# The shared expert's down weights in a two-layer MoE decoder step: a slot of the down ring at passes 24 and 25 instead of passes 1 and 2

## The chip, the core and the metric

The kernel runs on one core of a Trainium2 chip. A core has five engines that run their own instruction streams and meet through semaphores: TensorE (PE in the rows; PEld are its weight loads), VectorE (DVE), ScalarE (ACT), GpSimd (POOL) and SyncE (SP), which here only issues transfers. Weights lie in HBM and are brought into SBUF by DMA; matmul results go to PSUM. The metric is the device time of one execution in microseconds (us), lower is better.

## What is computed

One inference step of a decoder trunk of two layers, for 256 prompt tokens and 8 x 8 sample tokens (320 in all, width 1024). Each layer has a token mixer (window attention in layer 0, gated linear attention in layer 1) and then a mixture of experts, which takes most of the time:

```python
scores = sigmoid(x @ router_w)                       # 64 experts
... group-limited top 8 of 64 -> eidx, weights w
routed = sum over the 8 chosen e: w_e * (silu(x @ wg[e]) * (x @ wu[e])) @ wd[e]
shared = (silu(x @ swg) * (x @ swu)) @ swd           # one expert that every token uses
return routed + shared
```

An expert has a gate-and-up matrix (wg and wu, 1024 x 512 together, 2 MiB in float32) and a down matrix (wd, 256 x 1024, 1 MiB). The shared expert has the same sizes: shared_up is its gate and up, **shared_down** (swd) its down matrix. All 64 experts are loaded once per layer.

## The kernel before

**Passes.** Experts are sorted by how many tokens they drew and run in 28 passes per layer, two or three experts side by side in a pass (`PASSES`; passes 1, 2, 7, 13, 16, 21, 26 and 27 hold three). `LOAD_ORDER` numbers the 64 experts in the order of the passes; "item 34" below is number 34 of that order, counted from 0. Pass 14 holds items 32 and 33, pass 15 items 34 and 35, pass 24 items 54 and 55, pass 25 items 56 and 57, pass 26 items 58 to 60, pass 27 items 61 to 63. In a pass TensorE does the gate-and-up product (L2029), a part of the token gathering for the next batch of passes (L1931), turns the hidden values (L2055), adds the pass before into the sums of the tokens (L1959, L1961), and does the down product (L2079). Its last down product raises `y_full`.

**Rings.** Gate-and-up weights go through a ring of six slots (`gu_ring`), down weights through a ring of five (`dn_ring`, `NDN = 5`). A slot may be loaded again when the pass that read it is done: `gu_full` frees slots of the first ring, `y_full` those of the second.

**Who issues.** SyncE issues all gate-and-up loads in the order of the passes (L1612); each waits for its slot. SyncE also issues the first down loads (L1596 for items 0 and 1, L1615 for items below `DN_EARLY`) and those of the last pass (L1621). All other down loads are issued by ScalarE (L2127), at the end of the pass that frees the slot, behind that pass's two copies of the down result (L2121). So there are two hardware queues: SyncE's (q1) with the 2 MiB loads, ScalarE's (q10) with the 1 MiB loads, and each serves its loads in order.

**The shared expert.** Its gate and up run before the passes (L1723). Its down weights are loaded by SyncE (L1603) while the routing is computed, into the fifth slot of the down ring; only four slots are left for early items (`DN_EARLY = 4`). Its down product, in three parts of 128, 128 and 64 tokens (`shared_down`, L2007), runs in passes 1 and 2: the first part behind the down product of pass 1, the other two between the gate-and-up product and the turning of pass 2. The last part raises `shd_used`, and item 8 may then take the slot. From item 9 on, item i takes the slot of item i - 5.

Of the kernel before, what the change touches and what calls it, by code (L numbers as in the profile page):

```python
# [40 lines left out]
GH, DK, DV = 4, 128, 256  # L41
NE, FF = 64, 256
NGRP = 8
NGU, NDN, DN_EARLY = 6, 5, 4
DN_PLACE = (3, 4, 0, 1, 2)
NFIX = 2
EPS = 1e-6
# [43 lines left out]

PASSES = [pass_plan(l) for l in range(2)]
NP = len(PASSES[0])
BATCHES = (2, 4, 4, 4, 4, 4, 4, 2)
BATCH_OF = [(q, j) for q, n in enumerate(BATCHES) for j in range(n)]
BATCH_START = [sum(BATCHES[:q]) for q in range(len(BATCHES))]
# [144 lines left out]
def decoder_step(nc, a, debug=None):  # L241
    with ExitStack() as ctx:
# [25 lines left out]
        lay, const_range, _ = const_layout()  # L268
# [1294 lines left out]
        order = sb("order", [P, NE], I32)  # L1563
        excess = sb("excess", [P, 2], I32)
        last_dn = [None] * NDN
        gu_of, dn_of = {}, {}

        def expert_slots(l):

            for r in LOAD_ORDER[l]:  # L1570
                s = units[0] % NGU
                units[0] += 1
                i = LOAD_ORDER[l].index(r)
                d = i % DN_EARLY if i < 2 * DN_EARLY else (i + 1) % NDN
                used = (S["shd_used"], l + 1) if i == 2 * DN_EARLY else None if i < DN_EARLY else last_dn[d]
                slot_in[s].n += 16
                down_in[d].n += 16
                gu_of[(l, r)] = (s, slot_in[s].n, last_item[s])
                dn_of[(l, r)] = (d, down_in[d].n, used)
                last_item[s] = (S["gu_full"], l * NP + pass_of[l][r] + 1)  # L1580
                last_dn[d] = (S["y_full"], 2 * (l * NP + pass_of[l][r] + 1))

        def expert_stream(l, dn_ring):

            w_up, wd = a["moe_up"][l], a["moe_wd"][l]

            @block.sync
            def _(sp):
                if l == 0:
                    sp.wait_ge(*attention_read[0])  # L1590
                else:
                    sp.wait_ge(*states_out[0])
                    stored.wait(sp)
                for r in range(NFIX):
                    d = dn_of[(l, r)][0]
                    sp.dma_start(dn_ring[:, DN_PLACE[d], :], wd[r].rearrange("(p f) n -> p (f n)", p=P)).then_inc(down_in[d].h, 16)  # L1596
                for r in range(NFIX):
                    s, _, used = gu_of[(l, r)]
                    sp.wait_ge(*used)
                    sp.dma_start(gu_ring[:, s, :], w_up[r]).then_inc(slot_in[s].h, 16)  # L1600
                normed(sp, 2 * l + 1)
                stored.wait(sp)
                sp.dma_start(dn_ring[:, DN_PLACE[NDN - 1], :], a["shared_down"][l]).then_inc(down_in[NDN - 1].h, 16)  # L1603
                sp.wait_ge(S["order_full"], l + 1)
                for i, r in enumerate(LOAD_ORDER[l]):
                    if i < NFIX:
                        continue
                    e = sp.value_load(order[0:1, r:r + 1], min_val=0, max_val=NE - 1)
                    s, _, used = gu_of[(l, r)]
                    if used:  # L1610
                        sp.wait_ge(*used)
                    sp.dma_start(gu_ring[:, s, :], w_up[e]).then_inc(slot_in[s].h, 16)  # L1612
                    if i < DN_EARLY:
                        d = dn_of[(l, r)][0]
                        sp.dma_start(dn_ring[:, DN_PLACE[d], :], wd[e].rearrange("(p f) n -> p (f n)", p=P)).then_inc(down_in[d].h, 16)  # L1615

                for r, _ in PASSES[l][NP - 1]:
                    e = sp.value_load(order[0:1, r:r + 1], min_val=0, max_val=NE - 1)
                    d, _, used = dn_of[(l, r)]
                    sp.wait_ge(*used)  # L1620
                    sp.dma_start(dn_ring[:, DN_PLACE[d], :], wd[e].rearrange("(p f) n -> p (f n)", p=P)).then_inc(down_in[d].h, 16)  # L1621
# [14 lines left out]
        def moe(l):  # L1636
            with ExitStack() as c:
                dn_ring = sb("dn_ring", [P, NDN, DNW], c=c)
                down_in[NDN - 1].n += 16
                shd_n = down_in[NDN - 1].n  # L1640
                expert_slots(l)
                expert_stream(l, dn_ring)
                htok = sb("htok", [P, 2, 2, D], F32R, c=c)
                htok2 = sb("htok2", [P, D], F32R, c=c)
# [3 lines left out]
                ovh = sb("ovh", [P, 2, T], c=c)  # L1648
                sg_, sg_n = shared_in[l]
                shw = item(sg_)  # L1650
                shd = dn_ring[:, DN_PLACE[NDN - 1], :].rearrange("p (f n) -> p f n", f=2)

                def step(ins):
                    settled(nc.vector, ins)
# [268 lines left out]
                def _(pe):  # L1923
# [87 lines left out]
                    for p in range(NP):  # L2011
# [31 lines left out]

                        turns = list(enumerate(fills))
                        fill_some(turns[:3])
                        if p == 2:
                            shared_down(1, (0,))
                            shared_down(1, (1,))
                            shared_down(2, (0, 1)).then_inc(S["shd_used"], 1)
# [23 lines left out]
                        for half in range(2):  # L2073
# [5 lines left out]
                                    last = pe.matmul((W1, W2)[half][o:o + n, :], hTs[:, f, o:o + n],  # L2079
                                                     dn_ring[:, DN_PLACE[dn_of[(l, r)][0]], w0:w0 + 512], start=(f == 0), stop=(f == 1))  # L2080
                            last.then_inc(S["y_full"], 1)
                        if p == 1:
                            pe.wait_ge(down_in[NDN - 1].h, shd_n)
                            shared_down(0, (0,))
                            shared_down(0, (1,))
                    rest_pe(pe, left)
# [4 lines left out]
                def _(act):  # L2091
# [15 lines left out]
                    for p in range(NP):  # L2107
                        if p == NP - 1:
                            left = any_left(act)
                        q = BATCH_OF[p][0]  # L2110
                        act.wait_ge(S["gu_full"], l * NP + p + 1)
                        act.activation(sg[:, :], W0[:, 0:FF], ACT.Silu).then_inc(S["silu_full"], 1)  # L2112
                        for f in fills_in(p)[::2]:
                            fill_out(q + 1, f)
                        act.wait_ge(S["tr_full"], l * (NP + 1) + p + 2)
                        act.copy(hTs[:, :, :], W0[:, 0:FF].rearrange("p (f s) -> p f s", s=P)).then_inc(S["hT_full"], 1)  # L2116
                        if last_of(p):
                            weights_out(q + 1)
                        for half in range(2):
                            act.wait_ge(S["y_full"], 2 * (l * NP + p) + half + 1)  # L2120
                            act.copy(yhi[:, half, :], (W1, W2)[half]).then_inc(S["y_high"], 1)  # L2121
                        for r in LOAD_ORDER[l][DN_EARLY:len(LOAD_ORDER[l]) - len(PASSES[l][NP - 1])]:
                            d, _, used = dn_of[(l, r)]
                            if used == (S["y_full"], 2 * (l * NP + p + 1)) or (p == 2 and used == (S["shd_used"], l + 1)):
                                e = act.value_load(order[0:1, r:r + 1], min_val=0, max_val=NE - 1)
                                act.wait_ge(*used)
                                act.dma_start(dn_ring[:, DN_PLACE[d], :], a["moe_wd"][l][e].rearrange("(p f) n -> p (f n)", p=P)).then_inc(down_in[d].h, 16)  # L2127
# [466 lines left out]
```

## Time and profile before

| | us |
|---|---|
| median of 3 runs (1441.85 to 1442.69) | 1442.52 |
| the profiled execution | 1440.6 |
| its span in the profile | 1438.8 |
| busy TensorE in the span | 1397.9 (97%) |
| busy VectorE, ScalarE, GpSimd | 437.5, 317.1, 48.1 |
| passes of layer 0, first gate-and-up product to last down product | 247 to 707 |
| passes of layer 1 | 956 to 1418 |

The span is what the profile covers; the execution's time is 1.8 us longer. TensorE is busy nearly all the time, and so are the DMA engines during the passes, so busy shares alone do not tell which of the two sets the end. That is read from the waits, from the times of single transfers, and from the bytes moved in a stretch.

### The profile page before, as it was taken

The page shows a single profiled execution, that of the slowest core. Times are in us where ns is not written, and L with a number is a line of the kernel's source. Part 1 is how long each engine was busy: PE and PEld are TensorE (multiplying, and loading weights), DVE is VectorE, ACT ScalarE, POOL GpSimd, SP SyncE. Part 2 cuts the span into 40 slices and gives each one's busy share as a digit, 9 for nine tenths or more (in the row PEclk, how much of TensorE's full clock was granted, in tenths as well). Part 3 has the DMA queues.
Part 4 walks back from the last instruction along what each step waited for, and adds up shares of the span by engine and source line. Part 5 has one row for each costly group of instructions (what it writes and reads, how often), then busy time and mean ns, then how long its engine had stood idle before and what let it go on. Part 6 is the DMA issues. An engine that isn't in the chain of part 4 may idle for free.

```text
span 1438.8 us, 20775 instructions
## 1 busy us (share of the span) xinstructions
PE 1397.9 (97%) x8288; PEld 707.9 (49%) x8288; DVE 437.5 (30%) x1161; ACT 317.1 (22%) x746; POOL 48.1 (3%) x86
## 2 busy tenths in 40 slices
PE   7999999999999999999999999999999999999997
PEld 3345656444444444544465456564444445444433
DVE  1146435312221222221345143442122212132114
ACT  2134323111111111111345122411111111111113
POOL 0100301000000000000100010010000000000000
PEclk9999999999999999999999999999999999999999
DMA  9999528999999999999972246289999999999992
GB/s 392 386 383 427 218 94 321 391 402 427 411 424 427 419 426 426 423 427 425 406 298 118 117 161 239 91 361 404 405 427 417 425 420 422 425 425 424 426 419 88
DMA packets 48003, 509.52 MB, mean 354 GB/s; under 512 B 5809, under 2 KB 6209, under 8 KB 8321
## 3 DMA queue, kind: packets, MB, share of 16 engines
q1 hardware_dynamic: 27728, 370.42, 61.9%
q10 hardware_dynamic: 16416, 119.54, 20.1%
q0 software_dynamic: 3760, 18.20, 3.4%
q8 instruction: 68, 1.11, 0.3%
q14 instruction: 31, 0.25, 0.0%
HBM read 499.10 MB, written 11.01 MB: 355 GB/s over the span
## 4 chain that ended last, share of the span: by engine, by line
PE 87%; DMA 5%; DVE 3%; ACT 3%; issue 1%; ACTq 0%; SPq 0%; DVEq 0%
PE bank L2029 25%; PE banks L2079 13%; PE banks L1931 10%; PE banks L442 5%; DMA s_dn_ring<-in_moe_wd_dram 4%; PE ybank L1959 3%; PE banks L1119 3%; PE banks L1959 3%; PE bank L1961 3%; PE bank L504 2%; PE ybank L1723 1%; PE banks L1723 1%; DMA s_gu_ring<-in_ada_w_dram 1%; PE banks L697 1%; PE banks L1124 1%; PE banks L671 1%
## 5 line engine op out<-in xcount | busy, mean ns | idle before, releaser
L2029 PE MATMUL bank<-s_gu_ring,s_hbuf 128*32 128x512 f32 (+1 forms) x2688 | 395.3, 593 | 0.9 <-DVE s_hbuf L2160 0.9
L2029 PEld LDWEIGHTS bank<-s_gu_ring,s_hbuf 128*32 128x32 f32 (+1 forms) x2688 | 122.2, 119 | 264.7 <-issue 264.7
L2079 PE MATMUL banks<-s_dn_ring,s_hTs 128*32 128x512 f32 (+1 forms) x1344 | 205.9, 602 | 4.9 <-DMA s_dn_ring<-in_moe_wd_dram 4.9
L2205 DVE TENSOR_TENSOR s_ylo<-banks,s_yhi 128x512 fp32r<-128x512 f32 x112 | 77.5, 692 | 327.0 <-ACT s_yhi L2121 327.0
L1931 PE MATMUL banks<-s_sel,s_htok 128*128 128x512 f32 (+1 forms) x640 | 144.8, 374 | 0.5 <-issue 0.5
L1931 PEld LDWEIGHTS banks<-s_sel,s_htok 128*128 128x128 f32 x640 | 106.3, 188 | 60.7 <-issue 44.3
L2121 ACT CAST s_yhi<-banks 128x512 fp32r<-128x512 f32 x112 | 65.7, 586 | 303.3 <-PE banks L2079 303.3
L2079 PEld LDWEIGHTS banks<-s_dn_ring,s_hTs 128*32 128x32 f32 (+1 forms) x1344 | 56.8, 119 | 123.9 <-issue 123.2
L2200 DVE SCALAR_TENSOR_TENSOR s_hh<-s_sg,s_wsl,bank 128x256 f32<-128x256 f32 x56 | 26.9, 480 | 287.2 <-ACT s_sg L2112 287.2
L2112 ACT ACTIVATE s_sg<-bank 128x256 f32<-128x256 f32 x56 | 21.6, 385 | 364.0 <-PE bank L2029 364.0
L2160 DVE COPY s_hbuf<-banks 128x512 f32<-128x512 f32 (+1 forms) x60 | 39.4, 656 | 96.0 <-PE banks L1931 96.0
L1119 PE MATMUL banks<-s_gu_ring,s_hbuf 128*128 128x512 f32 x128 | 55.9, 593 | 0.5 <-DVE s_rs L1439 0.5
L2095 ACT COPY s_hbuf<-banks 128x512 f32<-128x512 f32 (+1 forms) x60 | 33.5, 559 | 57.9 <-PE banks L1931 57.9
L1959 PE MATMUL ybank<-s_yhi,s_gt 128*128 128x512 f32 x108 | 38.7, 439 | 0.0
L1119 PEld LDWEIGHTS banks<-s_gu_ring,s_hbuf 128*128 128x128 f32 x128 | 24.2, 191 | 29.1 <-issue 28.2
L504 PE MATMUL bank<-s_gu_ring,s_condT 128*32 128x512 f32 x288 | 35.5, 605 | 0.6 <-DMA s_gu_ring<-in_ada_w_dram 0.6
L2116 ACT COPY s_hTs<-bank 128x256 f32<-128x256 f32 x56 | 20.9, 373 | 64.0 <-PE bank L2055 43.1
L442 PE MATMUL banks<-s_qk,s_gu_ring 128*128 128x320 f32 x128 | 34.9, 433 | 0.0
L442 PE MATMUL banks<-s_hbuf,s_gu_ring 128*128 128x320 f32 x128 | 34.9, 433 | 0.0
L1959 PE MATMUL ybank<-s_ylo,s_gt 128*128 128x512 f32 x108 | 33.9, 395 | 0.0
L1959 PE MATMUL banks<-s_yhi,s_gt 128*128 128x512 f32 x108 | 33.9, 395 | 0.0
L1959 PE MATMUL banks<-s_ylo,s_gt 128*128 128x512 f32 x108 | 33.6, 392 | 0.0
(463 smaller groups left out, 1452.9 us busy)
## 6 DMA issues: line engine op xcount, KB each, us to landing
s_gu_ring<-in_moe_up_dram SPq DMA_DIRECT2D x128, 2048.0 KB, 16.2
s_dn_ring<-in_moe_wd_dram ACTq DMA_DIRECT2D x114, 1024.0 KB, 17.0
s_gu_ring<-in_ada_w_dram SPq DMA_DIRECT2D x24, 2048.0 KB, 14.3
s_dn_ring<-in_moe_wd_dram SPq DMA_DIRECT2D x14, 1024.0 KB, 11.2
s_gu_ring<-in_win_dram SPq DMA_DIRECT2D x6, 2048.0 KB, 12.0
s_gu_ring<-in_wqkv_dram SPq DMA_DIRECT2D x6, 1024.0 KB, 19.5
s_gu_ring<-in_wo_dram SPq DMA_DIRECT2D x2, 2048.0 KB, 20.5
s_gu_ring<-in_shared_up_dram SPq DMA_DIRECT2D x2, 2048.0 KB, 10.7
```

The lines of the kernel that those rows point to most:

```text
L442: last = pe.matmul(b[:, 0:T], item(slot)[:, k, (m % 4) * P:(m % 4 + 1) * P], src[:, k, :], start=(k == 0), stop=(k == KC - 1))
L504: last = pe.matmul(ada_bank(n)[32 * j:32 * j + 32, :], condT[:, k, lo:lo + 32], item(s)[:, k, :], start=(x == 0 and kk == 0), stop=(ends_g ...
L1119: last = pe.matmul(b[:, :], hT[:, k, t0:t0 + P], w[:, k, :], start=(k == 0), stop=(k == KC - 1))
L1931: last = pe.matmul(b[:, width * x:width * x + width], w[:, m * P:(m + 1) * P], sel[:, s, 0:width], start=(n == 0), stop=(n == 4))
L1959: last = pe.matmul(acc[(t, half)], g[:, t * P:(t + 1) * P], y[:, half, :], start=(p == 0 and y is yhi), stop=False)
L1961: last = pe.matmul(bank[6][:, :], g[:, 320 - 64 * half:448 - 64 * half], y[:, half, :], start=(p == 0 and y is yhi and half == 0), stop=False)
L2029: last = pe.matmul(W0[o:o + n, :], tokens_of(p, k)[:, o:o + n], w[:, k, :, :], start=(k == 0), stop=(k == KC - 1))
L2079: last = pe.matmul((W1, W2)[half][o:o + n, :], hTs[:, f, o:o + n], dn_ring[:, DN_PLACE[dn_of[(l, r)][0]], w0:w0 + 512], start=(f == 0), st ...
L2095: act.copy(fill_target(q, f), fill_source(q, f)).then_inc(S["fill_act"], 1)
L2121: act.copy(yhi[:, half, :], (W1, W2)[half]).then_inc(S["y_high"], 1)
L2160: dve.tensor_copy(fill_target(q, f), fill_source(q, f)).then_inc(S["fill_dve"], 1)
L2205: dve.tensor_tensor(ylo[:, half, :], (W1, W2)[half], yhi[:, half, :].bitcast(F32), ALU.subtract).then_inc(S["y_low"], 1)
```

## The change

The shared expert's down weights become an item of the down ring. They stand behind the experts of passes 0 to 24 (ahead of item 56), take the slot of item 51, and are issued by ScalarE at the end of pass 22. Their products run in pass 24 (first part, behind its down product) and pass 25 (the other two). All five slots are free for early items: item 4 is now issued early by SyncE. Items 56 to 60 each take the slot of the ring's entry five places before, so item 60 waits for the last product of the shared expert (`shd_used`), and ScalarE issues it at the end of pass 25.

```diff
-NGU, NDN, DN_EARLY = 6, 5, 4
+NGU, NDN, DN_EARLY = 6, 5, 5
...
+SHD_PASS = 24
...
+            shd_at = sum(len(experts) for experts in PASSES[l][:SHD_PASS + 1])
             for r in LOAD_ORDER[l]:
...
-                d = i % DN_EARLY if i < 2 * DN_EARLY else (i + 1) % NDN
-                used = (S["shd_used"], l + 1) if i == 2 * DN_EARLY else None if i < DN_EARLY else last_dn[d]
+                if i == shd_at:
+                    d = i % NDN
+                    down_in[d].n += 16
+                    shd_of.append((d, down_in[d].n, last_dn[d]))
+                    last_dn[d] = (S["shd_used"], l + 1)
+                d = (i + (i >= shd_at)) % NDN
+                used = None if i < NDN else last_dn[d]
...
-                sp.dma_start(dn_ring[:, DN_PLACE[NDN - 1], :], a["shared_down"][l]).then_inc(down_in[NDN - 1].h, 16)
...
-                        if p == 2:
+                        if p == SHD_PASS + 1:
                             shared_down(1, (0,))
                             shared_down(1, (1,))
                             shared_down(2, (0, 1)).then_inc(S["shd_used"], 1)
...
-                        if p == 1:
-                            pe.wait_ge(down_in[NDN - 1].h, shd_n)
+                        if p == SHD_PASS:
+                            pe.wait_ge(down_in[shd_d].h, shd_n)
                             shared_down(0, (0,))
                             shared_down(0, (1,))
...
+                        if shd_of[l][2] == (S["y_full"], 2 * (l * NP + p + 1)):
+                            act.wait_ge(*shd_of[l][2])
+                            act.dma_start(dn_ring[:, DN_PLACE[shd_d], :], a["shared_down"][l]).then_inc(down_in[shd_d].h, 16)
                         for r in LOAD_ORDER[l][DN_EARLY:len(LOAD_ORDER[l]) - len(PASSES[l][NP - 1])]:
                             d, _, used = dn_of[(l, r)]
-                            if used == (S["y_full"], 2 * (l * NP + p + 1)) or (p == 2 and used == (S["shd_used"], l + 1)):
+                            if used == (S["y_full"], 2 * (l * NP + p + 1)) or (p == SHD_PASS + 1 and used == (S["shd_used"], l + 1)):
```

TensorE, layer 0, in the kernel before: the end of pass 1 (L2079) and the first half of pass 2. L2007 is the shared expert's down product.

```order
L2079 MATMUL banks<-s_dn_ring,s_hTs 32x512 x16
L2007 MATMUL ybank<-s_dn_ring,s_ovh 128x512 x4
L2029 MATMUL bank<-s_gu_ring,s_hbuf 32x512 x32
L1931 MATMUL banks<-s_sel,s_htok 128x512 x4
L1931 MATMUL banks<-s_sel,s_htok_0 128x512
...
L2007 MATMUL banks<-s_dn_ring,s_ovh 128x512 x4
L2007 MATMUL bank<-s_dn_ring,s_ovh 64x512 x4
L2055 MATMUL bank<-s_cst,s_hh 128x128 x2
```

In the changed kernel the two L2007 places are gone here: L2029 follows L2079, and L2055 follows L1931.

TensorE, layer 0, in the changed kernel: the end of pass 24 and the first half of pass 25. The same lines have other numbers there: L2085 is the down product, L2013 the shared expert's, L2035 gate-and-up, L1937 the gathering, L2061 the turning.

```order
L2085 MATMUL banks<-s_dn_ring,s_hTs 64x512 x8
L2013 MATMUL ybank<-s_dn_ring,s_ovh 128x512 x4
L2035 MATMUL bank<-s_gu_ring,s_hbuf 64x512 x16
L1937 MATMUL banks<-s_sel,s_htok 128x256 x4
L1937 MATMUL banks<-s_sel,s_htok_0 128x256
...
L2013 MATMUL banks<-s_dn_ring,s_ovh 128x512 x4
L2013 MATMUL bank<-s_dn_ring,s_ovh 64x512 x4
L2061 MATMUL bank<-s_cst,s_hh 128x128 x2
```

The three products moved as they are, by 23 passes.

ScalarE, layer 0, in the changed kernel: the end of pass 22 and all of pass 23. L2127 copies the down result, L2134 reads the expert's number, L2130 and L2136 issue down loads.

```order
L2127 CAST s_yhi<-banks 128x512 x2
L2130 DMA s_dn_ring<-in_shared_down_dram 128x2048
L2134 TENSOR_LOAD s_order
L2134 ISA x2
L2136 ISA
L2136 DMA s_dn_ring<-in_moe_wd_dram 128x2048
L2118 ACTIVATE s_sg<-bank 128x256
L2101 COPY s_hbuf<-banks 128x256
L2122 COPY s_hTs<-bank 128x256
```

In the kernel before, this place issues items 55 and 56; now it issues the shared expert's weights and, behind them, item 55.

## Rows read from the trace of the kernel before

**Rows 1.** The page, part 1: engine, busy us, share of the span, instructions.

```profile
PE 1397.9 (97%) x8288; PEld 707.9 (49%) x8288; DVE 437.5 (30%) x1161; ACT 317.1 (22%) x746; POOL 48.1 (3%) x86
```

**Rows 2.** TensorE's waits, whole span: who waited for whom, us, times, longest.

```profile
PE banks L2079 <- DMA s_dn_ring<-in_moe_wd_dram: 4.9, 2, 2.5
```

**Rows 3.** Timeline of TensorE at pass 26 of both layers: start, us, instruction, [idle before <- releaser].

```profile
690.12 3.64 PE L2079 MATMUL banks<-s_dn_ring,s_hTs 128*32 128x512 f32 x32 [2.42 <-DMA s_dn_ring<-in_moe_wd_dram]
...
1399.23 1.82 PE L2079 MATMUL banks<-s_dn_ring,s_hTs 128*32 128x512 f32 x8 [2.52 <-DMA s_dn_ring<-in_moe_wd_dram]
```

**Rows 4.** The chain that ended last: start, us, what; the longest transfer in layer 0.

```profile
663.78 26.21 DMA s_dn_ring<-in_moe_wd_dram
```

**Rows 5.** Timeline of TensorE, layer 0, end of pass 1 and pass 2.

```profile
282.51 3.70 PE L2007 MATMUL ybank<-s_dn_ring,s_ovh 128*128 128x512 f32 x8
286.14 7.07 PE L2029 MATMUL bank<-s_gu_ring,s_hbuf 128*32 128x512 f32 x64
...
295.56 3.59 PE L2007 MATMUL banks<-s_dn_ring,s_ovh 128*128 128x512 f32 x8
...
300.96 0.50 PE L2055 MATMUL bank<-s_cst,s_hh 128*128 128x128 f32 x2
```

**Rows 6.** SyncE in layer 0: the shared expert's early load, and item 63's load.

```profile
214.74 0.33 SPq L1603 DMA_DIRECT2D s_dn_ring<-in_shared_down_dram  x1
...
L1621 SPq DMA_DIRECT2D s_dn_ring<-in_moe_wd_dram x1: 338/338/338, 694.0 to 694.0; - x1
...
DMA to landing us min/median/max: 4.9/4.9/4.9
```

**Rows 7.** Timeline of TensorE: the down products of passes 24, 25 (layer 0) and 24 (layer 1).

```profile
658.34 3.65 PE L2079 MATMUL banks<-s_dn_ring,s_hTs 128*64 128x512 f32 x16
...
673.85 3.65 PE L2079 MATMUL banks<-s_dn_ring,s_hTs 128*64 128x512 f32 x16
...
1367.37 3.65 PE L2079 MATMUL banks<-s_dn_ring,s_hTs 128*64 128x512 f32 x16
```

**Rows 8.** Windows of layer 0: busy us of each engine, granted clock, DMA share, GB/s.

```profile
252.00:260.00 8.00, 8.00 (x38) 4.91 (x36) 1.65 (x3) 1.83 (x4) 0.00 (x0) 1.00 0.88 339
264.00:280.00 16.00, 16.00 (x118) 9.06 (x112) 2.65 (x7) 2.06 (x5) 0.00 (x0) 1.00 0.96 385
308.00:316.00 8.00, 8.00 (x70) 3.01 (x63) 1.39 (x4) 0.83 (x2) 0.00 (x0) 1.00 0.91 339
316.00:640.00 324.00, 324.00 (x2047) 151.99 (x2046) 77.52 (x189) 50.76 (x105) 0.00 (x0) 1.00 1.01 423
```

**Rows 9.** The DMA view from 547 to 691 us: packets, MB, mean rate.

```profile
DMA packets 5634, 61.18 MB, mean 425 GB/s; under 512 B 631, under 2 KB 631, under 8 KB 631
```

**Rows 10.** Single down loads of layer 0, items 33, 34, 41, 55: issue time, us to landing.

```profile
L2127 ACTq DMA_DIRECT2D s_dn_ring<-in_moe_wd_dram x1: 345/345/345, 471.4 to 471.4; - x1
...
DMA to landing us min/median/max: 10.1/10.1/10.1
...
L2127 ACTq DMA_DIRECT2D s_dn_ring<-in_moe_wd_dram x1: 345/345/345, 487.6 to 487.6; - x1
...
DMA to landing us min/median/max: 11.1/11.1/11.1
...
L2127 ACTq DMA_DIRECT2D s_dn_ring<-in_moe_wd_dram x1: 345/345/345, 535.7 to 535.7; - x1
...
DMA to landing us min/median/max: 11.7/11.7/11.7
...
L2127 ACTq DMA_DIRECT2D s_dn_ring<-in_moe_wd_dram x1: 344/344/344, 633.1 to 633.1; - x1
...
DMA to landing us min/median/max: 19.5/19.5/19.5
```

**Rows 11.** The same of layer 1: item 34.

```profile
L2127 ACTq DMA_DIRECT2D s_dn_ring<-in_moe_wd_dram x1: 344/344/344, 1196.6 to 1196.6; - x1
...
DMA to landing us min/median/max: 11.3/11.3/11.3
```

More of the change, by code:

```diff
@@ L1565, in decoder_step @@
         last_dn = [None] * NDN
+        shd_of = []
         gu_of, dn_of = {}, {}
         def expert_slots(l):
+            shd_at = sum(len(experts) for experts in PASSES[l][:SHD_PASS + 1])
             for r in LOAD_ORDER[l]:
@@ L1638, in moe @@
                 dn_ring = sb("dn_ring", [P, NDN, DNW], c=c)
-                down_in[NDN - 1].n += 16
-                shd_n = down_in[NDN - 1].n
                 expert_slots(l)
+                shd_d, shd_n, _ = shd_of[l]
                 expert_stream(l, dn_ring)
@@ L1650, in moe @@
                 shw = item(sg_)
-                shd = dn_ring[:, DN_PLACE[NDN - 1], :].rearrange("p (f n) -> p f n", f=2)
+                shd = dn_ring[:, DN_PLACE[shd_d], :].rearrange("p (f n) -> p f n", f=2)
                 def step(ins):
```

## The prediction

> **What bounds the kernel now.** I read the page first: TensorE is busy 97% of the span [rows 1]. The stages between the passes do not see this change, so the question is who sets the end of the 28 passes of each layer. Next the waits of TensorE: in both layers together it waits for down weights only twice, 4.9 us in all [rows 2]. The timeline places both at the down product of pass 26, 2.42 us in layer 0 and 2.52 us in layer 1 [rows 3]; the reader is to see that every other pass finds its weights in time. The chain of waits names the late transfer: a down load of layer 0 that took 26.2 us from its issue [rows 4]. It is item 60, issued behind pass 24. So the passes run at TensorE's pace up to pass 25, and the transfers, which take as much time as TensorE, lose by 2.5 us at the end. The two are nearly level, and what counts is how far each is ahead of the other at each pass.
>
> **What the change does to TensorE.** The first part of the shared expert's product takes 286.14 - 282.51 = 3.63 us in pass 1, the other two 300.96 - 295.56 = 5.40 us in pass 2 [rows 5], together 9.03 us. The same instructions run in passes 24 and 25, so the sum of TensorE's work does not change. But passes 3 to 24 come 9.03 us earlier, until the work is paid back behind the down product of pass 24. In pass 2 the two parts stood where the hidden values are made; the gathering ahead of them (L1931) covers that in all other passes too, so nothing new is exposed. Every slot is freed 9.03 us earlier from pass 2 on, and every load is needed 9.03 us earlier up to pass 24.
>
> **What it does to the transfers.** Taken away: one 1 MiB load by SyncE at 214.74, while the routing is computed and the DMA engines have time [rows 6]. Nothing waits behind it on SyncE but the wait for the routing. Added: one early load (item 4) on SyncE behind the gate-and-up load of item 4; SyncE's next step after that is a wait for a slot of the other ring, and the gate-and-up loads behind it are needed in pass 2, which starts at 286.14 [rows 5], far later. I cost both at nothing. ScalarE issues as many down loads as before, 57 up to item 60: item 4 is gone, the shared expert's has come. Its added wait at the end of pass 22 is for the same down product that the copies ahead of it waited for, so nothing is queued behind it.
>
> What costs is the order on ScalarE's queue. The shared expert's load is issued at the end of pass 22, ahead of item 55, though TensorE wants item 55 first, in pass 24. In the kernel before, the down product of pass 24 starts at 658.34 in layer 0 and 1367.37 in layer 1 [rows 7]; without a stall it now starts at 649.31 and 1358.34. When does item 55 land?
>
> I start from a load whose issue TensorE sets. In the early passes the DMA engines have gaps: 339, 385 and 339 GB/s where the long stretch has 423 [rows 8]. From about 547 us both queues always have work, 425 GB/s [rows 9]. Between them, item 33 was issued at 471.4 and landed 10.1 us later at 481.5, and item 34 was issued only at 487.6, because its slot came free then [rows 10]: ScalarE's queue had run empty. With five slots it cannot hold a larger lead, whatever was won earlier. So in the changed kernel item 34 is issued 9.03 us earlier, at 478.6, and lands after the same 11.1 us [rows 10] at 489.7. In layer 1 it is 1196.6 - 9.03 + 11.3 = 1198.9 [rows 11]. Behind it on the queue come items 35 to 54, the shared expert and item 55: 22 loads.
>
> The pace of the queue when both have work: an expert is 2 + 1 MiB = 3.146 MB, which at 425 GB/s [rows 9] is 7.40 us per down load. Item 41 was issued at 535.7 and landed 11.7 later at 547.4 [rows 10], item 60 at 663.78 + 26.21 = 689.99 [rows 4]: 19 steps in 142.6 us, 7.50 us each. From item 34 (498.7) to item 55 (633.1 + 19.5 = 652.6) [rows 10] there are 21 steps of 7.33 us, with places where the other queue ran dry and left more to this one. In the changed kernel the gate-and-up loads are issued 9 us earlier and run dry less, so I take 7.46, between the first two values.
>
> Layer 0: 489.7 + 22 x 7.46 = 653.8, and 0.1 us from landing to product [rows 3, 4] makes 653.9, which is 4.6 us after 649.31. Layer 1: 1198.9 + 164.1 + 0.1 = 1363.1, which is 4.8 us after 1358.34. At 7.33 the stalls are 1.8 and 2.0 us, at 7.50 5.5 and 5.7.
>
> **What is late next.** A stall in pass 24 pushes all that follows, and the old stall in pass 26 is swallowed by it, unless item 60 comes later than before. Now item 60 waits for the last shared product and is issued at the end of pass 25. In the kernel before that end is 673.85 + 3.65 = 677.5 [rows 7]; with the stall it is 682.1, and with some 0.7 us for the copy between them the issue is near 682.8 (the second load behind pass 24 came 663.78 - 661.99 = 1.8 us after its end [rows 4, 7], the only one behind pass 25 needs less). Pass 26 wants it at 687.7 + 4.6 = 692.3 (690.12 less the wait of 2.42 [rows 3], plus the stall). It has 9.5 us. Alone, a down load takes 4.9 us [rows 6]; first on its queue beside a busy one, 11.1 us [rows 10]. At that point only the last gate-and-up load and items 61 and 62 are left beside it, so three down loads, 3.1 MB at 425 GB/s or 7.4 us, plus the 2.5 us by which 4.9 exceeds one load's 2.47, make 9.9: a stall of 0.4 us, with ends of 0 and 1.6.
>
> **The sum.** Stalls after: 4.6 + 4.8 + 2 x 0.4 = 10.2 us. Stalls before: 4.9 us. The change costs 5.3 us. The profiled execution took 1440.6 us, 1.8 more than its span, so it would take 1445.9; the median of the runs is 1442.52, 1.9 above that execution, and with the same 5.3 us I forecast **1447.8**. With a pace of 7.33 the sum is 1.8 + 2.0 + 0.8 - 4.9 = -0.3, or 1442.2; with 7.50 and 1.6 us at pass 26 it is 5.5 + 5.7 + 3.2 - 4.9 = +9.5, or 1452.0.
>
> **The rivals.**
>
> 1. *The transfers win back what they lose early, and the kernel gets faster.* The gaps [rows 8] are worth (423 - 339) x 8 + (423 - 385) x 16 + (423 - 339) x 8 = 2.0 MB, against 1.05 MB that is added to the busy stretch. If the earlier issues close these gaps and the lead lasts, all stalls go: 1442.5 - 4.9 = 1437.6. It decides at item 55: it must land by 649.3, 3.3 us earlier than in the kernel before, with one more load ahead of it on its queue. Against it: the queue that ran dry before item 34 [rows 10], which a lead does not outlive. The Trainium skill ("DMA: Bandwidth & Descriptors", section "Issuing engines are not separate DMA queues") says that transfers of all issuing engines run on the same 16 DMA engines and interleave, so that spreading them saves only issue time. The trace agrees that they share, with 425 GB/s for both queues together [rows 9]; by that rule alone only bytes would count, and this rival would hold. This rival has a chance of 0.07.
>
> 2. *Nothing changes.* Item 60 stays the 57th load of ScalarE's queue, and what is late at pass 24 is made up by less at pass 26; at the pace of 7.33 this gives 1442.2, within 0.2%. For it: 7.33 is the pace that the trace has over nearly the same items. Against it: it includes dry places of the other queue. Chance 0.20.
>
> 3. *Item 60 becomes the late one.* If its load took the 19.5 to 26.2 us of items 55 and 60 [rows 4, 10] and not 9.9, it would land at 702 to 709, 10 to 17 us late in each layer: some 1465 to 1480. Those latencies were queues of two or three loads ahead; here items 58 and 59 have landed. Chance 0.03.
>
> **How the numbers follow.** The forecast has 0.70, the rivals 0.07, 0.20 and 0.03. A measurement of this kernel can tell about 0.2% (2.9 us) from no change. The forecast's own cases (pace 7.40 to 7.50) lie above that but for its lower edge, so slower has 0.70 + 0.03 less 0.03, which is 0.70; the same 0.23; faster 0.07. The range goes from 1442.0, rival 2, to 1452.0, the upper end of the pace.
>
> **What would show it.** TensorE's waits for down weights in the changed kernel: about 4.7 us at the down product of pass 24 in each layer, on item 55, and less than 2 us at pass 26; no wait in passes 1 to 23, and pass 3 starting 9.0 us earlier. No wait at the shared product itself in pass 24, since its load lands ahead of item 55. The windows from 308 to 316 us should show a rate near 423 GB/s. I am wrong if pass 24 does not wait (rival 1 or a faster pace), if a pass between 14 and 23 already waits (the queue is later than I think, and the time with it), or if the wait stands at pass 26.

## The result: 1448.24 us against 1442.24 us, and the profile after

Six runs of each kernel on one chip: the changed kernel takes 1448.24 us in the median (1447.49 to 1450.44), the kernel before 1442.24 us (1440.63 to 1445.68). The ratio is 1.0040, with a 95% interval from 1.0027 to 1.0053, so the change costs between 3.9 and 7.6 us; the difference of the medians is 6.0. The forecast was 1447.8 us, 5.3 us slower.

The profiled execution of the changed kernel took 1450.44 us, with a span of 1448.6. It is the longest of its six runs, 2.2 us above their median, while the profiled execution of the kernel before lay 1.6 us below its median. So the two traces differ by 9.8 us where the medians differ by 6.0. The places can be read from the traces, their sum only to some 4 us.

TensorE's waits over the whole span come first (who waited for whom, us, times, longest); this line answers to [rows 2].

```profile
PE banks L2085 <- DMA s_dn_ring<-in_moe_wd_dram: 9.8, 2, 5.5
```

There are two waits for down weights again, but twice as long: 9.8 us in place of 4.9. The timeline of TensorE in layer 0 (start, us, instruction, idle before it and its releaser; L2085 is the down product, L2013 the shared expert's, L2035 the gate-and-up product) tells where the first one stands. It answers to [rows 3, 7].

```profile
655.14 6.50 PE L2085 MATMUL banks<-s_dn_ring,s_hTs 128*64 128x512 f32 x16 [5.54 <-DMA s_dn_ring<-in_moe_wd_dram]
661.57 3.70 PE L2013 MATMUL ybank<-s_dn_ring,s_ovh 128*128 128x512 f32 x8
665.20 7.09 PE L2035 MATMUL bank<-s_gu_ring,s_hbuf 128*64 128x512 f32 x32
...
673.51 3.60 PE L2013 MATMUL banks<-s_dn_ring,s_ovh 128*128 128x512 f32 x8
677.04 1.94 PE L2013 MATMUL bank<-s_dn_ring,s_ovh 128*64 128x512 f32 x8
...
682.80 3.65 PE L2085 MATMUL banks<-s_dn_ring,s_hTs 128*64 128x512 f32 x16
...
696.58 3.64 PE L2085 MATMUL banks<-s_dn_ring,s_hTs 128*32 128x512 f32 x32
```

The reader is to see three things. The wait stands at the down product of pass 24. The shared product behind it, and pass 26 (696.58), wait for nothing. And the sixteen instructions of pass 24's down product take 6.50 us, where the same sixteen take 3.65 in pass 25. In layer 1 it reads the same:

```profile
1370.47 5.35 PE L2085 MATMUL banks<-s_dn_ring,s_hTs 128*64 128x512 f32 x16 [4.29 <-DMA s_dn_ring<-in_moe_wd_dram]
1375.75 3.70 PE L2013 MATMUL ybank<-s_dn_ring,s_ovh 128*128 128x512 f32 x8
```

Why the product behind the wait is slow is told by windows of the changed kernel (busy us of each engine, then TensorE's granted clock, the DMA share and GB/s). The second and third row lie on these two products:

```profile
882.40:886.00 3.60, 3.00 (x9) 2.45 (x10) 0.55 (x2) 0.62 (x2) 0.89 (x1) 0.55 0.35 122
655.00:661.00 6.00, 5.86 (x14) 1.91 (x16) 1.05 (x2) 0.59 (x1) 0.00 (x0) 0.51 1.02 430
1371.00:1374.30 3.30, 3.30 (x10) 1.14 (x8) 0.00 (x0) 0.49 (x1) 0.00 (x0) 0.50 0.99 420
```

Behind each wait TensorE is busy, but at a granted clock of 0.5, the lower level of 1.2 GHz, after 2.4 GHz in the passes ahead. The stretch at the lower level is 6.8 us long in layer 0, from about 654.1, a us before the wait's end, to 660.9; in layer 1 it is 3.4 us. It costs 6.50 - 3.65 = 2.85 us and 5.35 - 3.65 = 1.70 us. The Trainium skill ("TensorE: Matmul & The Clock Gate", section "What's actually happening") has the clock set, between these two levels, by how busy the engine has just been; the rows agree at these two places, since both falls come at the end of a wait of over 4 us. The kernel before had one such stretch, behind its wait in layer 1 [rows 3]: that down product, with its 32 instructions, takes 5.34 us in all, where 3.64 is usual, a loss of 1.70 us.

```profile
1399.23 5.34 PE L2079 MATMUL banks<-s_dn_ring,s_hTs 128*32 128x512 f32 x32 [2.52 <-DMA s_dn_ring<-in_moe_wd_dram]
```

Its wait in layer 0, 2.42 us, was followed by none. The first row of the windows is a third place at the lower level, between the passes of the two layers, which the kernel before does not have in its trace; no wait just ahead of it is longer than 0.62 us. It comes back below.

Last the late transfer. In the chain of waits (start, us, what) the load of item 55 takes the place of that of item 60 [rows 4]; single issues on ScalarE's queue (line, operation, ns, time of the issue; us to landing) show the shared expert's load ahead of it at 623.6 and item 55 at 624.7, 30.3 us long.

```profile
624.66 30.34 DMA s_dn_ring<-in_moe_wd_dram
655.00 0.14 issue
655.14 6.50 PE banks L2085 x16
```

```profile
L2130 ACTq DMA_DIRECT2D s_dn_ring<-in_shared_down_dram x1: 345/345/345, 623.6 to 623.6; - x1
...
DMA to landing us min/median/max: 24.0/24.0/24.0
...
L2136 ACTq DMA_DIRECT2D s_dn_ring<-in_moe_wd_dram x1: 340/340/340, 624.7 to 624.7; - x1
...
DMA to landing us min/median/max: 30.3/30.3/30.3
```

So in layer 0 the shared expert's weights lay in SBUF at 647.6, and TensorE stood until 655.0 for the load queued behind them.

### The profile page after: what moved, and what is told of

Read it like the earlier page. It is cut to its first block, busy times and chain, and to the rows that moved or that the text cites. A ratio compares the mean times of both kernels' runs of the same rounds, so it can differ in the third digit from the quotient of the medians.

```text
span 1448.6 us, 20771 instructions
## 1 busy us (share of the span) xinstructions
PE 1401.6 (97%) x8288; PEld 708.1 (49%) x8288; DVE 437.6 (30%) x1161; ACT 317.1 (22%) x746; POOL 48.1 (3%) x86
## 4 chain that ended last, share of the span: by engine, by line
PE 87%; DMA 5%; DVE 3%; ACT 3%; issue 1%; SPq 0%; ACTq 0%; DVEq 0%
PE bank L2035 25%; PE banks L2085 13%; PE banks L1937 9%; PE banks L443 5%; DMA s_dn_ring<-in_moe_wd_dram 4%; PE ybank L1965 3%; PE banks L1120 3%; PE banks L1965 3%; PE bank L1967 3%; PE bank L505 2%; PE ybank L1729 1%; PE banks L1729 1%; DMA s_gu_ring<-in_ada_w_dram 1%; PE banks L698 1%; PE banks L1125 1%; PE banks L672 1%
## 5 line engine op out<-in xcount | busy, mean ns | idle before, releaser
L2035 PE MATMUL bank<-s_gu_ring,s_hbuf 128*32 128x512 f32 (+1 forms) x2688 | 395.3, 593 | 0.9 <-DVE s_hbuf L2169 0.9
L2035 PEld LDWEIGHTS bank<-s_gu_ring,s_hbuf 128*32 128x32 f32 (+1 forms) x2688 | 121.4, 119 | 265.6 <-issue 265.6
L2085 PE MATMUL banks<-s_dn_ring,s_hTs 128*32 128x512 f32 (+1 forms) x1344 | 208.8, 604 | 9.8 <-DMA s_dn_ring<-in_moe_wd_dram 9.8
L1937 PE MATMUL banks<-s_sel,s_htok 128*128 128x512 f32 (+1 forms) x640 | 144.8, 374 | 0.5 <-issue 0.5
L1937 PEld LDWEIGHTS banks<-s_sel,s_htok 128*128 128x128 f32 x640 | 106.3, 188 | 60.7 <-issue 44.3
L2127 ACT CAST s_yhi<-banks 128x512 fp32r<-128x512 f32 x112 | 65.7, 586 | 311.1 <-PE banks L2085 311.1
L2085 PEld LDWEIGHTS banks<-s_dn_ring,s_hTs 128*32 128x32 f32 (+1 forms) x1344 | 57.5, 120 | 130.8 <-issue 130.0
```

The lines of the kernel that those rows point to most:

```text
L1937: last = pe.matmul(b[:, width * x:width * x + width], w[:, m * P:(m + 1) * P], sel[:, s, 0:width], start=(n == 0), stop=(n == 4))
L2035: last = pe.matmul(W0[o:o + n, :], tokens_of(p, k)[:, o:o + n], w[:, k, :, :], start=(k == 0), stop=(k == KC - 1))
```

## The experiments

My theory after the result: item 55 is late because the shared expert's load stands ahead of it on ScalarE's queue, and the time lost there is the longer wait and, behind it, the clock. The rivals: that TensorE's head start of 9 us does it alone, since every load is wanted 9 us earlier; that the slow product behind the wait has another cause than the idle time; and that the extra load harms at any place on the queue. All runs are timed against the kernel before on the same chip (median 1442.21 us for the first three below and for item 60 moved alone, 1442.35 us for the others). The changed kernel was not run again beside them; where a run is compared with its 1448.24 us, the comparison goes by kernels before that differ by 0.1 us.

### One place on the queue

The shared expert's block of ScalarE is put behind the loop that issues the down loads, so that item 55 goes first:

```diff
-                        if shd_of[l][2] == (S["y_full"], 2 * (l * NP + p + 1)):
-                            act.wait_ge(*shd_of[l][2])
-                            act.dma_start(dn_ring[:, DN_PLACE[shd_d], :], a["shared_down"][l]).then_inc(down_in[shd_d].h, 16)
                         for r in LOAD_ORDER[l][DN_EARLY:len(LOAD_ORDER[l]) - len(PASSES[l][NP - 1])]:
...
+                        if shd_of[l][2] == (S["y_full"], 2 * (l * NP + p + 1)):
+                            act.wait_ge(*shd_of[l][2])
+                            act.dma_start(dn_ring[:, DN_PLACE[shd_d], :], a["shared_down"][l]).then_inc(down_in[shd_d].h, 16)
```

> The changed kernel with one thing undone: at the end of pass 22 ScalarE issues item 55 first and the shared expert's down weights behind it. Bytes, slots and TensorE's order stay. Theory (place on ScalarE's queue): item 55 lands one step of about 7.4 us earlier, near 647.6 in layer 0, and the 5.5 and 4.3 us waits for it at pass 24 go. The shared weights land where item 55 landed (655.0), 1 to 2 us after the down product of pass 24 is done, so a wait of 0.5 to 2 us shows there, and up to 1.5 us at pass 26. Without long waits TensorE's clock falls less. Time 1441 to 1444. Rival (bytes): what costs is the 1 MB more in the busy stretch, 2.5 us per layer, wherever it is queued: the waits only move, and the time stays within 1 us of 1448.2.

It took 1439.03 us, a ratio of 0.9982 (0.9969 to 0.9994): 3.2 us under the kernel before and 9.2 under the changed one, below what I had expected. TensorE in layer 0:

```profile
649.21 3.65 PE L2085 MATMUL banks<-s_dn_ring,s_hTs 128*64 128x512 f32 x16
...
653.53 3.70 PE L2013 MATMUL ybank<-s_dn_ring,s_ovh 128*128 128x512 f32 x8 [0.67 <-DMA s_dn_ring<-in_shared_down_dram]
...
689.75 3.64 PE L2085 MATMUL banks<-s_dn_ring,s_hTs 128*32 128x512 f32 x32 [1.14 <-DMA s_dn_ring<-in_moe_wd_dram]
```

The down product of pass 24 no longer waits, the shared product waits 0.67 us, pass 26 1.14, and in this trace no product of the passes runs at the lower clock (four of the twelve runs have a lower mean clock than its 0.998, down to 0.994). The two issues beside each other show the exchange:

```profile
L2133 ACTq DMA_DIRECT2D s_dn_ring<-in_moe_wd_dram x1: 340/340/340, 624.0 to 624.0; - x1
L2136 ACTq DMA_DIRECT2D s_dn_ring<-in_shared_down_dram x1: 545/545/545, 624.4 to 624.4; - x1
...
DMA to landing us min/median/max: 22.1/25.6/29.1
```

The first of the two lands at 646.1, the second at 653.5, 7.4 us apart, and only the second place is too late for item 55. So one place on the queue is worth 9.2 us of the time, some 4.6 per layer, the waits and the clock behind them together. It shows too that the lead won in passes 1 and 2 does reach pass 24: item 55 lands 6.5 us earlier than in the kernel before (652.6 [rows 10]).

### TensorE kept busy through the wait

Twenty small products that nobody reads, of two instructions each, are put ahead of the wait in pass 24, in the changed kernel; no transfer is touched.

```diff
+                        if p == SHD_PASS:
+                            keep_awake(pe, W0, 20)
                         for r in ranks:
```

> The changed kernel plus 20 small products (128x128, results unused) on TensorE in pass 24, ahead of its wait for down weights: some 4.7 us of work inside the wait of 4.3 to 5.5 us. Theory (the idle gap costs twice): in the changed kernel the granted clock is at half for some 7 us in layer 0 and 3.4 us in layer 1 just behind the gap, and the down product of pass 24 takes 6.5 and 5.35 us where it took 3.65. With the gap filled the clock stays up, the product takes 3.65 again and the time falls by 3 to 4.5 us, to 1444 to 1445. Rival (the fall of the clock has nothing to do with the gap): the products stay slow and the time stays at 1448.2 or rises by up to 1 us.

It took 1444.21 us, ratio 1.0013 (1.0004 to 1.0022), 4.0 us under the changed kernel. The timeline in layer 0, then a window on the product:

```profile
649.02 4.63 PE L424 MATMUL bank<-s_cst 128*128 128x128 f32 x40
653.79 3.65 PE L2087 MATMUL banks<-s_dn_ring,s_hTs 128*64 128x512 f32 x16
657.38 3.70 PE L2013 MATMUL ybank<-s_dn_ring,s_ovh 128*128 128x512 f32 x8
```

```profile
653.00:661.00 8.00, 7.85 (x30) 3.16 (x29) 1.95 (x5) 1.17 (x2) 0.00 (x0) 1.00 1.01 427
```

The products fill 4.63 us in each layer, 9.3 us in place of 9.8 us of waiting, so the time that passes there is nearly the same. But the down product takes 3.65 us again at a clock of 1.00. That the slow product behind the wait is a matter of the idle time ahead of it, and not of its operands or of the transfers beside it, is thereby shown: the two losses add to 4.55 us by the traces, and the time falls by 4.0 us, of which some 0.5 are the shorter stop. The mean granted clock says the same of all runs: it is 0.993 to 0.995 in the six of the changed kernel and 0.996 to 0.998 in the twelve of this one.

### The shared expert's load on the other queue

SyncE issues it, ahead of the gate-and-up load of item 58; ScalarE's block goes.

```diff
+SHD_BEFORE = 58
...
+                    if i == SHD_BEFORE:
+                        sp.wait_ge(*shd_of[l][2])
+                        sp.dma_start(dn_ring[:, DN_PLACE[shd_of[l][0]], :], a["shared_down"][l]).then_inc(down_in[shd_of[l][0]].h, 16)
```

> The changed kernel with the shared expert's down load issued by SyncE, ahead of its gate-and-up load of item 58, when pass 22 has freed the slot, and not by ScalarE. Same bytes, same slot, about the same time of issue; ScalarE's queue is one load shorter ahead of item 55. Theory (place on ScalarE's queue): 21 steps and not 22 from item 34 to item 55, which lands near 647.6, in time; no wait at pass 24, at most 2.5 us at pass 26, time 1440 to 1443.5. Rival (bytes): the same 1 MB delays everything behind it by 2.5 us in each layer, wherever it stands; waits of about 5 us per layer remain, time 1446 to 1448.

It took 1438.22 us, ratio 0.9965 (0.9951 to 0.9978), 10.0 us under the changed kernel and again below what I had expected. The load was issued at 623.7, as before, and landed 25.6 us later. Item 55 no longer stood behind it, and no product waited for the gate-and-up load that now did:

```profile
PE banks L2089 <- DMA s_dn_ring<-in_moe_wd_dram: 3.0, 2, 1.6
```

Both waits that are left (1.40 and 1.55 us) are at pass 26. The same megabyte at nearly the same moment costs nothing when it is in the queue of the gate-and-up weights. The Trainium skill ("DMA: Bandwidth & Descriptors", section "Queues, rings and completion order") has each DMA engine serve in turn the queues that have work; the rows agree (from 625 to 647 us the changed kernel's two queues moved 428 and 426 packets), and what counts for item 55 is the work ahead of it on its own queue.

### Without the head start

Behind the down product of pass 2 the changed kernel gets small products of 8.97 us, nearly the 9.03 us that were moved away, so that passes 3 to 24 come when they came in the kernel before.

```diff
+                        if p == 2:
+                            keep_awake(pe, W0, 39)
```

> The changed kernel plus 39 small products (128x128, results unused, about 9.0 us) on TensorE behind the down product of pass 2: the head start of 9.03 us that passes 3 to 24 won is taken away again, and the order of loads stays. Question: which part of the wait at pass 24 (5.5 and 4.3 us) comes from the extra load ahead of item 55, and which from the head start? Theory (mostly the extra load): issue and need of items 34 to 55 shift together, so the head start itself costs only by the two queues being busier; the wait at pass 24 shrinks to about 2 us (22 steps of 7.33 to 7.4 us from 498.7 give 660.0 to 661.5, wanted at 658.3). Rival (the head start is the cause): no wait at pass 24. Time, in either case mostly the added work: 1448.2 + 18 less 6 to 12, 1454 to 1460.

It took 1458.74 us, ratio 1.0113 (1.0094 to 1.0132), of which 17.9 us are the added products. In layer 0, pass 2 and pass 24:

```profile
298.65 8.97 PE L424 MATMUL bank<-s_cst 128*128 128x128 f32 x78
...
662.66 6.07 PE L2085 MATMUL banks<-s_dn_ring,s_hTs 128*64 128x512 f32 x16 [4.30 <-DMA s_dn_ring<-in_moe_wd_dram]
```

Pass 24 still waits, 4.30 us here and 1.77 in layer 1, 6.1 in all. So the head start alone is not the cause: of the 9.8 us of waiting, 6.1 stay without it, and 3.7 come with it. The shared expert's load ahead of item 55 is the greater part, and with that load behind item 55 the head start does no harm (3.4 us of waiting, in the first experiment). I had expected some 2 us in each layer; the mean is 3.0.

### The shared expert elsewhere, and item 60 at SyncE

Three more kernels ask whether the added load must cost at all. In the first, `SHD_PASS = 12` in place of 24, ahead of the place where ScalarE's queue runs dry:

> The changed kernel with the shared expert's item behind pass 12 and its products in passes 12 and 13. Theory (ScalarE's queue runs dry before item 34, and what was added or won earlier is forgotten there): the 1 MB is absorbed between passes 12 and 15, no wait at passes 12 to 14, and the end looks as in the kernel before, with a wait of about 2.4 us for item 60 at pass 26 in each layer; time 1441 to 1443. Rival (bytes): the extra 2.5 us of transfer per layer stay to the end, waits of about 5 us at pass 26, time 1446 to 1448.

It took 1439.23 us, ratio 0.9981 (0.9970 to 0.9991). That is below what I had expected.

```profile
PE banks L2085 <- DMA s_dn_ring<-in_moe_wd_dram: 3.8, 2, 2.2
```

Both waits are at pass 26 (2.19 and 1.64), with no fall of the clock in the passes. The extra load is absorbed ahead of the dry place, and item 60 lands at 690.0, as in the kernel before [rows 4].

In the second, `SHD_PASS = 20`, with the shared load behind the down load as in the first experiment:

> The shared expert's item behind pass 20, products in passes 20 and 21, with ScalarE issuing the experts' down loads of a pass ahead of the shared expert's. Theory: loads are issued 9 us early up to pass 20, so the queues hold no dry place after item 34, and the last passes profit; waits at passes 20 to 24 below 1 us, at pass 26 0 to 2.5 us. Time 1436.5 to 1441. Rival (bytes): as with pass 24, 1446 to 1448.

It took 1438.14 us, ratio 0.9979 (0.9964 to 0.9993), with 4.4 us of waiting, all of it at pass 26 (2.95 us in layer 0, where I had expected at most 2.5, and 1.45 in layer 1).

What both leave is the wait for item 60. One kernel takes it away in the kernel before: SyncE issues item 60's down load between the gate-and-up loads of items 61 and 62, and ScalarE skips it.

```diff
+DN_LATE, LATE_AT = 60, 61
...
+                    if i == LATE_AT:
+                        r2 = LOAD_ORDER[l][DN_LATE]
+                        e = sp.value_load(order[0:1, r2:r2 + 1], min_val=0, max_val=NE - 1)
+                        d, _, used = dn_of[(l, r2)]
+                        sp.wait_ge(*used)
+                        sp.dma_start(dn_ring[:, DN_PLACE[d], :], wd[e].rearrange("(p f) n -> p (f n)", p=P)).then_inc(down_in[d].h, 16)
```

> The kernel before with one load moved: item 60's down weights are issued by SyncE, between the gate-and-up loads of items 61 and 62, and not by ScalarE. Theory (ScalarE's queue is the late one): the waits of 2.4 and 2.5 us at pass 26 go, since item 60 need not stand behind items 57 to 59 and overtakes two 2 MB loads that are wanted later; pass 27 may wait 0 to 1 us for item 63's gate and up. Time 1436 to 1439, below the kernel before. Rival (the end of the passes is set by bytes alone): the wait moves whole to the gate and up of pass 27, and the time stays at 1442.

It took 1436.12 us, ratio 0.9953 (0.9939 to 0.9966). No down product waits; the gate-and-up product behind pass 26 now does, a little:

```profile
PE bank L2036 <- DMA s_gu_ring<-in_moe_up_dram: 1.5, 2, 1.0
```

The last kernel takes this together with the second (`SHD_PASS = 20`, shared load behind the down load, item 60 at SyncE):

> The run with the item behind pass 20, and besides item 60's down load issued by SyncE between the gate-and-up loads of items 61 and 62, as in the run that moved that load alone (1436.1). Theory: the wait for item 60 goes here too, and the gate and up of pass 27 are less late than the 0.7 us there: waits below 1.5 us in both layers together, time 1434.5 to 1437. Rival: nothing is left to win, and the two edits do not add: 1436 to 1438, with the waits at pass 27 as in that run or above.

It took 1433.86 us, ratio 0.9944 (0.9926 to 0.9961), the shortest of all and again below what I had expected: 8.5 us under the kernel before and 14.4 under the changed one. No product of its passes waits for a weight.

### The account over all kernels

The waits for weights within the passes, the loss behind them to the lower clock, and the added products, each in us and for both layers, against the kernel before (waits 4.9, clock 1.7); then the difference of the medians, and the difference of the two profiled executions (the one before took 1440.6 us).

| kernel | waits | clock | added | sum against before | medians | profiled |
|---|---|---|---|---|---|---|
| the change | 9.8 | 4.55 | 0 | +7.7 | +6.0 | +9.8 |
| item 55 first | 3.4 | 0 | 0 | -3.2 | -3.2 | -3.0 |
| TensorE kept busy | 0 | 0 | 9.3 | +2.6 | +2.0 | +2.5 |
| shared load by SyncE | 3.0 | 0 | 0 | -3.7 | -4.0 | -1.4 |
| without head start | 6.1 | 2.4 | 17.9 | +19.8 | +16.4 | +20.2 |
| pass 12 | 3.8 | 0 | 0 | -2.8 | -3.1 | -1.1 |
| pass 20 | 4.4 | 0 | 0 | -2.2 | -4.2 | -2.0 |
| item 60 by SyncE, in the kernel before | 1.5 | 0 | 0 | -5.1 | -6.1 | -3.3 |
| pass 20, item 60 by SyncE | 0 | 0 | 0 | -6.6 | -8.5 | -7.0 |

Waits and clock put the kernels in nearly the right order and come within 2 us of the medians, but for the kernel without head start (3.4 us). No median is above its sum, and most lie below. The sums are read from one trace each, so they belong to the profiled executions, and these they meet: within 0.5 us, but for the four kernels whose traces have the third place at the lower clock, between the layers (the change, shared load by SyncE, pass 12, item 60 by SyncE). From the start of the last down product of layer 0 to layer 1's first gate-and-up product these four take 254.1 to 254.2 us, the others 252.5 to 252.7; with 1.6 us more for that, all nine sums come within 0.7 us.

That the medians differ from the profiled executions is at least in part the clock, which differs between runs of one kernel. Of the 42 runs of the kernel before that stand beside the experiments, those with a mean granted clock of 0.997 took 1439.9 to 1441.7 us, those with 0.996 1441.5 to 1443.1, and those with 0.995 or 0.994 1442.0 to 1445.8. The trace of before is of a run at 0.997, and both medians are of runs at 0.996. One more stretch of 3.4 us at half the clock would lower the mean by 0.0012 and cost some 1.7 us, near the 1.6 us by which that trace lies below its median; this is an estimate, since no trace of such a run was kept. The 3.4 us of the kernel without head start look like the same: its profiled run, at 0.995, is the longest of four and 2.0 us above their median, the others have 0.997 and 0.998.

## Why the prediction was right

**The head start: right.** Pass 3 starts at 298.80 in layer 0, where the trace of before has 307.61. Pass 0 began 0.46 us later, so the lead is 9.27 us, where the prediction had 9.03.

```profile
295.34 3.64 PE L2085 MATMUL banks<-s_dn_ring,s_hTs 128*32 128x512 f32 x32
298.80 7.05 PE L2035 MATMUL bank<-s_gu_ring,s_hbuf 128*32 128x512 f32 x64
```

**Item 34 and the pace: right, to a tenth of a us and to a part of the landing.** The prediction had item 34 issued at 478.6 and landing after 11.1 us. The single issue reads:

```profile
L2136 ACTq DMA_DIRECT2D s_dn_ring<-in_moe_wd_dram x1: 339/339/339, 478.8 to 478.8; - x1
...
DMA to landing us min/median/max: 12.4/12.4/12.4
```

It landed at 491.15, 1.4 us later than worked out. From there to item 55 at 655.00 there are 22 steps of 7.45 us, against 7.46. In layer 1 it was issued at 1195.4 and landed 11.8 later, at 1207.2, and 22 steps of 7.41 lead to 1370.33; the times of that layer all lie some 8 us later than in the prediction, by what was lost ahead of them, the load and the product that wants it alike.

**Pass 24: the place right, the size nearly.** The prediction had 4.6 + 4.8 = 9.4 us of waiting; it is 5.54 + 4.29 = 9.83. The difference in layer 0 is mainly item 34's longer landing; in layer 1 the quicker pace, 7.41 us, made the wait shorter.

**Pass 26: no wait, where the prediction had 0.4 us in each layer.** Item 60 was issued at 687.2 and landed after 8.9 us, at 696.1, less than 0.5 us ahead of its product at 696.58. The prediction's 9.9 us were 1.0 too much. In those 8.9 us 3.15 MB were moved, just the three down loads of its sum. The issue came 4.4 us later than its 682.8, but together with the whole of pass 25, which the longer wait and the slow product of pass 24 had pushed back.

**The term that was missing: the clock.** The sum of the prediction knew waits only. Behind each of the longer waits a product ran at 1.2 GHz and lost 2.85 and 1.70 us by it, less the 1.70 that the kernel before lost already: 2.85 us net. It could have been read ahead: [rows 3] has only the first eight instructions of layer 1's pass 26, at 1.82 us, which is twice 0.91, what eight of 32 take in 3.64 us. That was a product at half clock behind a wait of 2.5 us, and I passed over it. With this term the traces give 4.9 + 2.85 = 7.7 us.

That the forecast still came out 0.4 us from the median, at +5.3 where the medians give +6.0, is thus partly luck: by the clocks on record above, a median run of the kernel before spends longer at the lower level than its trace does, which takes up part of the missing term. Two further pieces make up the 9.8 us between the traces: 0.46 us ahead of the passes of layer 0, and 1.55 us between the end of layer 0 and the start of layer 1 (254.06 us against 252.51). In this last stretch lies the third place at the lower clock, in the window from 882.4 to 886.0. The traces of the shared load by SyncE, of pass 12 and of item 60 by SyncE have it too, 6 to 8 us earlier as their layer 0 ends earlier, and those of the other kernels, the one before among them, don't. It follows no part of the edit that I can name. As the mean clock differs between runs of one kernel, it need not come from an edit at all; what brings it about was not settled.

**Rival 1, the transfers that win back the gaps: wrong for this change, nearly right with one place exchanged.** The windows that answer to [rows 8] read:

```profile
252.00:260.00 8.00, 8.00 (x38) 4.91 (x36) 1.45 (x6) 1.83 (x4) 0.00 (x0) 1.00 1.03 432
264.00:280.00 16.00, 16.00 (x118) 9.10 (x114) 2.72 (x7) 2.22 (x6) 0.00 (x0) 1.00 1.01 422
308.00:316.00 8.00, 8.00 (x60) 3.90 (x62) 2.15 (x4) 1.54 (x3) 0.00 (x0) 1.00 1.03 432
316.00:640.00 324.00, 324.00 (x2030) 152.08 (x2024) 77.93 (x192) 50.53 (x105) 0.00 (x0) 1.00 1.01 425
```

The gaps are closed: 432, 422 and 432 GB/s where there were 339, 385 and 339. The rival wanted just that, and the time rose all the same, since it decides at item 55, which came at 655.0 and was wanted at 649.6. With the order of two loads exchanged item 55 lands at 646.1, and the time is 1439.0, near the rival's 1437.6, though 3.4 us of waiting are left that it had gone. The prediction's own sum has this too: one step of 7.46 us less takes item 55 from 653.8 to 646.3. Its argument that a lead does not outlive the dry place before item 34 is true of the queue's lead over TensorE. TensorE itself came 9 us earlier there, and the queue behind it with it, as the sum had it; the argument, read as one against every gain of this kind, was too strong. What spoiled the change was one place on a queue.

**Rival 2**, nothing changes, wanted a pace of 7.33 us; it was 7.45 and 7.41. **Rival 3**, item 60 landing 10 to 17 us late, did not come: item 60 took 8.9 us.

## What to carry to other kernels

When a load is moved behind others on a queue that is always full, ask which load now stands ahead of which, and count it in landings: here one place is 7.4 us, and exchanging two loads, or giving one to the other queue, turned 6.0 us of loss into 3 to 4 us of gain. Order the loads by the time at which each is wanted, even where two are issued a microsecond apart. And when a wait is added in the middle of dense TensorE work, look in the trace of before for what products cost directly behind such waits, since the wait may not be the whole price.

## What the runs showed of the hardware

- **Waits of a few us are followed by products at 1.2 GHz, but not always.** In the passes, behind the waits for weights of 5.54 us (the change, layer 0) and 4.30 us (without head start, layer 0) the stretch at the lower level was 6.8 us long; behind 4.29 us (the change, layer 1) and 2.52 us (the kernel before, layer 1) it was 3.4 us. Behind 2.95 us (pass 20, layer 0), 2.42 us (the kernel before, layer 0) and all shorter ones there was none. In the kernel without head start it began at 660.7, while TensorE still waited. Between the layers of the changed kernel the clock fell for 3.4 us at 882.8, with no wait above 0.62 us just ahead. So the wait's length alone does not decide. Small products in the gap removed the effect in the passes (1444.21 us in place of 1448.24).
- **Runs of the kernel before differ in time as their mean granted clock does.** A clock of 0.997 goes with 1439.9 to 1441.7 us and 0.994 or 0.995 with 1442.0 to 1445.8; the six runs of the changed kernel, 0.993 to 0.995, show no such order. A time compared with a sum from a trace should be that of the traced run.
- **Two queues that both had work moved as many packets, not as many bytes.** These are SyncE's queue (q1) and ScalarE's (q10) in the changed kernel from 625 to 647 us: packets, MB, and the time of the packets as a share of 16 engines.

```profile
q1 hardware_dynamic: 428, 6.24, 66.7%
q10 hardware_dynamic: 426, 3.10, 33.9%
```

  So a down load of 1 MiB lands every 7.4 us on ScalarE's queue, beside SyncE's 2 MiB loads at the same pace, at 425 GB/s in all. Other mixtures of loads were not tried. Item 55, behind the loads ahead of it on its queue, took 30.3 us to land, and item 60, with none ahead of it there, 8.9 us.
